# Token numbers for the first item's rows, and the combine on TensorE, in a two-layer decoder step on Trainium2

## What is computed

```python
xn = _rmsnorm(x, W['norm_ffn_g'][i])
logits = xt @ w_router                      # 1088 x 8
top_v, top_i = lax.top_k(logits, 2)
top_w = jax.nn.softmax(top_v, axis=-1)
order = jnp.argsort(top_i.reshape(-1)); tok = order // 2
xs = xt[tok]                                # rows sorted by expert
h = silu(ragged_dot(xs, wg, sizes)) * ragged_dot(xs, wu, sizes)   # 1024 -> 3584
ys = ragged_dot(h, wd, sizes) * top_w[order]
x = x + zeros.at[tok].add(ys)
g = sigmoid(_rmsnorm(x, W['norm_ple_g'][i]) @ W['ple_w_gate'][i])
x = x + g * (p[i] @ W['ple_w_proj'][i])
```

## Time and profile before

| | us |
|---|---|
| median of the runs | 5131.51 |
| the profiled execution | 5134.26 |
| its span | 5132.7 |
| PE busy in the span | 4942.7 (96%) |
| DVE busy | 3395.0 (66%) |
| ACT busy | 1597.7 (31%) |
| POOL busy | 396.3 (8%) |

### The profile page before, as it was taken

How to read it: one execution, slowest core, us unless ns; L and a number is a source line. 1 busy time by engine, 2 the same in 40 slices (tenths; PEclk the granted TensorE clock), 3 DMA queues, 4 the chain that set the end, 5 groups by cost and what they waited for, 6 DMA issues and landing times. The chain is left out here.

```text
span 5132.7 us, 86754 instructions
## 1 busy us (share of the span) xinstructions
PE 4942.7 (96%) x33110; PEld 4876.0 (95%) x33111; DVE 3395.0 (66%) x5288; ACT 1597.7 (31%) x2290; POOL 396.3 (8%) x239
## 2 busy tenths in 40 slices
PE   8999999999999999999969999999999999999968
PEld 8999999999998999999959999999999999999968
DVE  5677757444556756876557777666667777876665
ACT  2112122111113311122224444333334444443333
POOL 3110101110102021110010000000000000000020
PEclk9999999999999999999979999999999999999989
DMA  3111111111111111111035554444446555654431
GB/s 105 44 45 41 41 40 42 50 41 44 46 41 44 41 56 40 47 41 42 29 117 177 177 175 165 160 146 160 150 148 207 187 192 184 199 185 150 146 125 42
DMA packets 398841, 527.64 MB, mean 103 GB/s; under 512 B 11944, under 2 KB 353494, under 8 KB 398504
## 3 DMA queue, kind: packets, MB, share of 16 engines
q1 hardware_dynamic: 359552, 460.75, 27.3%
q0 software_dynamic: 10912, 33.94, 2.0%
q10 hardware_dynamic: 28040, 28.63, 1.7%
HBM read 494.87 MB, written 28.39 MB: 102 GB/s over the span
## 5 line engine op out<-in xcount | busy, mean ns | idle before, releaser
L1596 DVE TENSOR_TENSOR WLO<-WRAW,WHI 128x1024 fp32r<-128x1024 f32 x866 | 1071.3, 1238 | 340.8 <-ACT WHI L1192 215.9
L658 PE MATMUL PS<-XHI,WHI 128*128 128x384 f32 (+1 forms) x3648 | 1203.2, 330 | 10.6 <-DVE XLO L1843 4.5
L660 PE MATMUL PS<-XHI,WLO 128*128 128x384 f32 (+1 forms) x3648 | 1197.6, 328 | 0.0
L659 PE MATMUL PS<-XLO,WHI 128*128 128x384 f32 (+1 forms) x3648 | 1197.1, 328 | 0.0
L1192 ACT ACTIVATE WHI<-WRAW 128x1024 fp32r<-128x1024 f32 x866 | 899.1, 1051 | 892.2 <-PE PS L773 602.8
L658 PE MATMUL PS<-XSH,WHI 128*128 128x232 f32 (+6 forms) x3584 | 1058.3, 295 | 12.5 <-DVEq L2300 12.2
L659 PE MATMUL PS<-XSL,WHI 128*128 128x232 f32 (+6 forms) x3584 | 1054.7, 294 | 0.0
L660 PE MATMUL PS<-XSH,WLO 128*128 128x232 f32 (+6 forms) x3584 | 1054.6, 294 | 0.0
L658 PEld LDWEIGHTS PS<-XHI,WHI 128*128 128x128 f32 x3648 | 691.7, 190 | 13.0 <-issue 5.2
L658 PEld LDWEIGHTS PS<-XSH,WHI 128*128 128x128 f32 x3584 | 678.7, 189 | 14.4 <-DVEq L2300 13.8
L659 PEld LDWEIGHTS PS<-XLO,WHI 128*128 128x128 f32 x3648 | 691.4, 190 | 0.9
(11 more groups left out here) (361 smaller groups left out, 5956.6 us busy)
## 6 DMA issues: line engine op xcount, KB each, us to landing
WRAW<-in_moe_w_gate SPq DMA_DIRECT2D x112, 1024.0 KB, 5.0
WRAW<-in_moe_w_up SPq DMA_DIRECT2D x112, 1024.0 KB, 5.0
WRAW<-in_moe_w_down SPq DMA_DIRECT2D x112, 1024.0 KB, 5.0
WRAW<-in_w_in SPq DMA_DIRECT2D x48, 1024.0 KB, 5.2
WRAW<-in_ffn_w_gate SPq DMA_DIRECT2D x11, 1024.0 KB, 5.2
WRAW<-in_ffn_w_up SPq DMA_DIRECT2D x11, 1024.0 KB, 5.3
WRAW<-in_ffn_w_down SPq DMA_DIRECT2D x11, 1024.0 KB, 4.9
XG<-sorted_rows POOLq DMA_DIRECT2D x18, 512.0 KB, 4.6
```

Source lines behind the costliest of these rows:

```text
L658: pe.matmul(PS[:, bank, 0:n], wh, hi(k), start=(k == 0), stop=False)
L659: pe.matmul(PS[:, bank, 0:n], wh, lo(k), start=False, stop=False)
L660: ins = pe.matmul(PS[:, bank, 0:n], wl, hi(k), start=False, stop=(k == KC - 1))
L1596: v.do(dve.tensor_tensor(WLO[s][:], raw_view(conv.n // 2 % RAW, conv.n % 2, kind), WHI[s][:].bitcast(F32), ALU.subtract), conv)
```

## The change

Both stages are rewritten; items themselves stay.

- **Router weights and constants.** GpSimd loads the router weights and writes the constants when the mixers' last merged products are evicted, and VectorE folds and splits them in the output projection (d == 3). High and low halves lie side by side in RWS (16 columns), so a block's logits need two products per chunk for three; TWIN adds the two halves when logits are transposed. Logits of two blocks stand ahead of the row sums.
- **Token rows.** `rows` multiplies XHI and XLO with an identity and accumulates, so XF goes. There are nine row buffers ROWT. ScalarE evicts each tile and stores it to a new DRAM tensor token_rows (XR).
- **Token numbers.** The expert of item 0 (the first one with more than 336 tokens, or else expert 0) is found from the counts. MASK compares each token's count so far with 336 ranks; the column sums of MASK on TensorE are, per rank, the number of the token with this rank. GpSimd gathers item 0's rows from XR by these numbers, then writes the padding, then scatters.
- **List.** The nine additions become four doubling steps; 13 levels become one comparison and one reduction; the slot selector is made once instead of three times.
- **Loop for further items.** One branch on the list's count passes it by on TensorE, ScalarE and VectorE, with branch hints. Waits for the first six scatters and the padding stand ahead of the first step; the clearing of EACC goes.
- **Combine.** VectorE builds diagonal matrices DG of the weights once; TensorE multiplies both gathered rows with them and adds them to x in a main bank. Squares are summed over columns by one-column products (`sum_squares`), so `stats` goes from the gate product. The embedding of layer 1 is loaded by GpSimd at the start of the items, and transposed and split before the first gathered rows. Gather buffers go from five pairs to three.

```diff
-GATHERS = 5
+GATHERS = 3
@@ SyncE
-                if j == 1:
-                    if l == 0:
-                        sp.wait_ge(S["evicted"], Q_LAST_DOWN)
-                    else:
-                        sp.wait_ge(S["ys_out"], n_items * 48 + 48)
-                        spacer(sp)
-                    load_p(sp, l)
+                if j == 1 and l == 0:
+                    sp.wait_ge(S["evicted"], Q_LAST_DOWN)
+                    load_p(sp, [PTOK[:, i, :] for i in range(NT)], l)
@@ GpSimd
-        g.wait_ge(S["phase_clear"], 1)
+        g.wait_ge(S["evicted"], Q_MIX1)
...
+        g.wait_ge(S["rows_written"], 16 * NT)
+        g.wait_ge(S["ids_ready"], 1)
+        for c, (r0, n) in enumerate(XBLK):
+            g.indirect_dma_start(XG[0:n, c, :], None, XR[0:NTOK, :], bass.IndirectOffsetOnAxis(ap=IDS[0:n, c:c + 1], axis=0)).then_inc(S["xg_ready"], 16)
         for j, (r0, n) in enumerate(XBLK):
-            g.dma_start(XS[PAIRS + r0:PAIRS + r0 + n, :], XG[0:n, j, :]).then_inc(S["scattered"], 16)
+            g.dma_start(XS[PAIRS + r0:PAIRS + r0 + n, :], ROWT[j][0:n, :]).then_inc(S["scattered"], 16)
+        g.wait_ge(S["places_ready"], 1)
         for j in range(NT):
             n = tokens(j)
-            if j == 0:
-                g.wait_ge(S["places_ready"], 1)
-            g.wait_ge(S["rows_ready"], j + 1)
             for k in range(2):
...
-        row = g.value_load(ITEMS[0:1, L_ROW + 1:L_ROW + 2], min_val=0, max_val=PAIRS)
-        for j, (r0, n) in enumerate(XBLK):
-            g.dma_start(XG[0:n, j, :], XS[bass.ds(row + r0, n), :]).then_inc(S["xg_ready"], 16)
+        load_p(g, PTILE, 1)
@@ TensorE, router
+                pe.wait_ge(S["rw_split"], 1)
+                logits(0)
+                logits(1)
+                stats()
+                logits(2)
+                rows(0)
...
+                for j in range(NT):
+                    n = tokens(j)
+                    pe.wait_ge(S["mask_ready"], j + 1)
+                    for c in (0, 2, 1):
+                        r0, w = XBLK[c]
+                        ins = pe.matmul(PS[0:w, b, c:c + 1], MASK[0:n, j, r0:r0 + w], ONES[0:n, 0:1], start=(j == 0 and c == 0),
+                                        stop=(j == NT - 1 and c == 1))
@@ TensorE, combine
+                p_columns([t[:] for t in PTILE])
+                sums = misc_bank()
+                def sum_squares(j):
+                    n = tokens(j)
+                    for h in range(2):
+                        pe.wait_ge(S["squared"], 2 * j + h + 1)
+                        for k in range(4):
+                            ins = pe.matmul(PS[0:n, sums, j:j + 1], TC[h][:, k, 0:n], ONES[:, 0:1], start=(h == 0 and k == 0), stop=(h == 1 and k == 3))
...
-                    pe.wait_ge(S["combined"], j + 1)
+                    pe.wait_ge(S[f"gathered{j % GATHERS}"], 32 * (j // GATHERS + 1))
...
-                            ins = pe.matmul(PS[:, b, k * P:k * P + n], YG[j % GATHERS][0][0:n, c0:c0 + P], IDF[0:n, 0:n], start=False, stop=(k == 3))
+                            for e in range(2):
+                                ins = pe.matmul(PS[:, b, k * P:k * P + n], YG[j % GATHERS][e][0:n, c0:c0 + P], DG[0:n, e, j, 0:n], start=False,
+                                                stop=(k == 3 and e == 1))
+                    if j:
+                        sum_squares(j - 1)
+                sum_squares(NT - 1).then_inc(m.next(), 1)
@@ ScalarE, router
+                    act.dma_start(XR[j * P:j * P + n, :], ROWT[j][0:n, :]).then_inc(S["rows_written"], 16)
@@ VectorE, router
+                for j in range(NT):
+                    v.do(dve.tensor_scalar(MASK[:, j, :], RANKS[:], C0[:, j:j + 1], None, ALU.is_ge), masked)
@@ VectorE, combine
-                combine(0)
+                for e in range(2):
+                    v.do(dve.tensor_tensor(DG[:, e], IDF[:].unsqueeze(1).to_broadcast([P, NT, P]), TW[:, e, :].unsqueeze(2).to_broadcast([P, NT, P]), ALU.mult))
+                v.sync()
+                dve.sem_inc(S["weights_ready"], 1)
+                p_columns(PTS[1], P_SPLIT[1])
```

More of the change, by code:

```diff
@@ L292, in build @@
+    DG = at("DG", [P, 2, NT, P], F32, PH + 24576)
+    TC = [at(f"TC{i}", [P, 4, P], F32, PH + 33792 + 2048 * i) for i in range(2)]
+    assert 8192 * GATHERS <= 24576 and NT <= 9
+    assert lo + 1920 <= PH + 80000 <= END - 4 * NE
+    XR = nc.dram_tensor("token_rows", [NTOK, D], F32).ap()
     XS = nc.dram_tensor("sorted_rows", [PAIRS + CAP, D], F32).ap()
@@ L367, in spacer, with load_p @@
         eng.sem_inc(S["spacer"], 1)
-    def load_p(q, l):
+    def load_p(q, tiles, l):
         for j in range(NT):
@@ L800, in _, with p_columns @@
         for l in range(DEPTH):
+            def p_columns(tiles):
+                pe.wait_ge(S[f"p_loaded{l}"], 16 * NT)
+                for c in range(2):
+                    for t0, n in BLOCKS:
+                        b = misc_bank()
+                        for j in range(t0 // P, -(-(t0 + n) // P)):
+                            w = tokens(j)
+                            ins = pe.transpose(PS[:, b, j * P - t0:j * P - t0 + w], tiles[j][0:w, c * P:(c + 1) * P], IDF[0:w, 0:w])
+                        ins.then_inc(m.next(), 1)
             if l:
@@ L1792, in _, with p_columns @@
         tok, stage = Count(S["tok_ready"]), Count(S["stage_full"])
+        def p_columns(whole, parts):
+            for c in range(2):
+                for t0, n in BLOCKS:
+                    ps = misc_ready()
+                    v.do(dve.tensor_copy(whole[:, c, t0:t0 + n], ps[:, 0:n]), m)
+            v.sync()
+            split_branch(whole, parts)
+            dve.sem_inc(S["p_ready"], 1)
         for t_, val in ((ONES, 1.0), (EPSC, EPS)):
@@ L2353, in _ @@
                 first, second, *middle, late, last = list(groups(MOE_GROUPS))
-                with dve.Fori(0, SLOTS - NE) as it:
-                    with dve.If(it < extras):
-                        st = looped(cs, it, per)
-                        kp[0] = LOOK
-                        for k in range(KC):
-                            prepare(k)
-                        step(*first)
-                        step(*second, between=lambda u: item_out(it, u) if u < len(XBLK) else None)
-                        for s in (*middle, late, last):
-                            step(*s)
-                        leave_items(cs, st, per, extras)
+                dve.br_lt(extras, 1, on_true="dve_firsts", on_false="dve_further").branch_hint(further)
+                with nc.body("dve_further", valid_engines=[dve.engine]):
+                    with dve.Fori(0, SLOTS - NE) as it:
+                        with dve.If(it < extras):
+                            st = looped(cs, it, per)
+                            kp[0] = LOOK
+                            for k in range(KC):
+                                prepare(k)
+                            dve.wait_ge(S["rows_gone0"], 96)
+                            dve.wait_ge(S["pads_clear"], 1)
+                            step(*first)
+                            step(*second, between=lambda u: item_out(it, u) if u < len(XBLK) else None)
+                            for s in (*middle, late, last):
+                                step(*s)
+                            leave_items(cs, st, per, extras)
+                    dve.br("dve_firsts")
+                nc.switch_bb("dve_firsts")
                 for k in range(KC):
                     prepare(k)
+                dve.wait_ge(S["rows_gone0"], 96)
+                dve.wait_ge(S["pads_clear"], 1)
                 with dve.Fori(0, NE) as e:
```

411 lines of the change are left out of this document (221 added, 190 removed).

## The result

| | before | after |
|---|---|---|
| median of the runs, us | 5130.53 (12 runs) | 5144.72 (12 runs) |
| the profiled execution, us | 5134.26 | 5140.98 |
| its span, us | 5132.7 | 5139.4 |

The changed kernel is slower: the ratio of its time to that of before is 1.0027, with a 95% interval of 1.002 to 1.0035, some 14 us. That is just within the 0.3% which the prediction called about what can be told from no change, but the interval excludes a ratio of 1. I had forecast 5125.1 us and a range of 5107 to 5137. The page gives these slices for the changed kernel (busy tenths, 40 slices of 128.5 us); they hardly differ from those of before, and PE was busy for 4982.9 us where it had 4942.7.

What follows compares the result with a forecast made beforehand. TensorE bounds the kernel, at 9 tenths in nearly every slice. Router 8.6 us saved less combine 2.2 us lost gives 6.4 us saved, from the median 5131.51 to 5125.1 us; range 5107 to 5137.

Steps and rivals of the forecast that it cites:

- counts read: Router: counts at 2629.5 to 2630, where before they were read at 2642.93.
- token numbers: Router: token numbers of item 0 at 2640 to 2644, taken as 2642.
- list ready: Router: list of items ready at about 2653 against 2663.9, 11 us early.
- third convert: Router: ScalarE's third convert of weight halves starts near 2681, as before, the list's 11 us being lost to the queue.
- Logits: Router: 48 products for 72, 8 to 9.1 us for 13.65, ending near 2620.
- Row products and masks on TensorE: Router: 144 row products, 9 to 17 us, fill the waits; 27 one-column mask products cost 5.9 us.
- Weights: Router queues: weights issued at 2658.2 in mid-scatter; indirect traffic moves 0.305 MB/us against 0.087 for weights.
- The rival of sharing alike by bytes: Router queues: weights flow at 0.19 MB/us, third convert ends at 2672.7, 9.6 us more saved: 5115.5; chance 0.33.
- the rival of the clock: Combine: whole loop at 1.2 GHz costs 40 us, 5165; half the tiles give 5145; chance 0.09.
- Behind the third convert: Router: the gain is what stood between third convert and item 0's rows, 8.6 us, bounds 5 and 11.
- far jump: Router, behind the third convert: the branch past six skipped loops waits for a fetch, 3 us lost: 5128; chance 0.13.
- Combine: Combine: TensorE is the bound at 7.0 us a tile; net 2.2 us slower, bounds 4 faster and 9 slower.

Runs made afterwards that it cites:

- numbers_short: The changed kernel with the masks' products of the first tile only, so token numbers are wrong; 5133.86 us, ratio 1.0009.
- list_first: The changed kernel with places and list made on VectorE before it waits for the token numbers; 5117.16 us, ratio 0.9973.
- combine_only: The kernel before with the whole new combine and the old router; 5132.02 us, ratio 1.0003.
- list_first_squares_on_dve: The changed kernel with the list made before the numbers and the squares reduced on VectorE; 5106.72 us, ratio 0.9951.
- masks_in_bf16: list_first_squares_on_dve with masks and ones in bfloat16, one record per product of the masks; 5107.85 us, ratio 0.9958.

## Why the prediction was wrong

Step by step, from M. Times of the forecast are turned into distances from M by taking off 2609.55.

| step | forecast | after |
|---|---|---|
| row products start (logits done) | M + 10.5 | M + 10.1 |
| counts read | M + 20 | M + 28.5 |
| token numbers | M + 32.5 | M + 50.7 |
| list ready | M + 43.5 | M + 61.7 |
| weights issued | M + 48.7 | M + 65.1 |
| third convert | M + 71.5 | M + 94.5 |
| first expert product | M + 84.2 | M + 106.9 |

- **Logits.** Right.
- **Row products and masks on TensorE: the step that failed.** I gave the row products bounds of 0.06 and 0.12 us each, 9 to 17 us, wrote that they "fill the waits", and took 5.9 us for the masks' products. They took 0.11 us each in the first ones and 0.21 us in nearly all the rest, some 27 us, and the masks' products 10.3 us. The sum is 37 us where I had 15 to 23. With 3 us of transposes and counts' products between them, TensorE works without a gap for the 40 us from the logits to the numbers. It was the bound of the router, and I treated it as filler; numbers_short shows that it was on the path. This step made the numbers 18.2 us late, and of the 22.7 us by which the first expert product missed its forecast the rest is the weights: 6.6 us more from issue to convert, less 1.8 us that SyncE issued sooner behind the list (3.4 us for 5.2) and 0.3 us behind the convert. Two things lay behind this misjudged sum: the bounds left out what stands between two products that each bring their own weights, and I put the rival of the clock into the combine, where it cost little, and not into the router. The Trainium skill (TensorE: Matmul & The Clock Gate, Wait — 56ns, not 53.3ns?) has 55.6 and 106.7 ns from start to start of back-to-back products of 128 columns at the two levels; the trace has twice that, 0.11 and 0.21 us, with new weights for each product. An estimate from these two figures would make the 144 products 8 to 15 us; at the trace's 0.11 and 0.213 us they would be 16 to 31.
- **Order on TensorE.** Four blocks of row products stand ahead of the counts' products, so VectorE waited 9.30 us for sums that TensorE could have made at 2620.9, and the counts were 8 us late. In this kernel it should have cost nothing, though no run moves it: the masks were ready at 2635.1, and TensorE came to them at 2641.99.
- **Order on VectorE.** I costed the list correctly at 11 us behind the numbers (2652.36 to 2663.34), but did not ask what it had to do there. It needs the counts alone. list_first shows that this order cost 33 us up to the first expert product. This was to be read from the diff and the place of the wait.
- **Weights.** The mechanism was right and is now shown: scatter 0.311 and weights 0.074 MB/us, where I had 0.305 and 0.087 from the earlier trace rows. 29.4 us from issue to third convert, where I had 22.8. When the weights began to flow, at 2668, only some 4.3 MB of 11.7 had gone, since the queue's first 15 us (from 2653) moved 0.29 MB/us and not the 0.378 I took: I had counted on 5.8 MB left and 7.4 were. The rival of sharing alike by bytes, with its 0.19 MB/us for the weights (chance 0.33), is refuted.
- **Behind the third convert.** Right: 12.4 us to the first expert product where before had 21.1, a gain of 8.7 for 8.6. The rows of item 0 did land ahead of the third convert, by 30 us (2666.06), but at M + 64.4, where I had M + 40 to 45. No far jump shows: ScalarE's next instruction (2697.20) follows the third convert without a gap. The 2.81 us that I called a fetch in full queues stand in the earlier trace rows with the releaser "remote", and no fetch is shown there, so no run shows that rival's price.
- **Combine.** Right in sum, and partly by luck: 1.4 and 0.8 us, and 3.1 in combine_only, for 2.2. First sum 21.4 us after the last expert product (21.9 forecast). The tile was 6.3 us and not 7.0; the end at low clock (5.36 us for 32 records of squares, where 16 take 1.84 warm) and the gate product, still cold, gave part of that back. The gate product did not start warm as I wrote: the granted clock was 0.50 in its first 4 us. It came 4.5 us later after E than before, where I had 7.2, and 3.1 us came back behind it, where I had 5.0; the two errors cancel.

The router is +12 to +14 us instead of -8.6. I forecast the right mechanism in the queues from a wrong time of arrival. The range was too narrow, since it let the numbers be late by 3 us at most. Two small misreadings carry no weight: from M to the first expert product before has 92.8 us, where I wrote 92.5, and the earlier trace rows shows 2.05 us for the row sums, where I wrote 1.97.

What stays open: why M itself moves by up to 8 us between profiles of kernels whose mixing layers differ little or not at all (the changed kernel's own two profiles have 2601.66 and 2605.96), and why the clock falls with one kind of product and not with the other.

## What to carry to other kernels

When work is moved onto an engine "into its waits", add up all of it from rows of the same kind, with their weights, at both clock levels, and compare the sum with the wait; and ask of each step behind a wait whether it needs what is waited for. Where a small transfer on the path and a large one off it share the queues, their order counts more than their times: the same weights were converted 16 us sooner, counted from M, when they were issued 4 us ahead of the gathers (list_first_squares_on_dve) than when they went out 0.8 us behind them (masks_in_bf16), and making the large one's trigger earlier can lose as much as it wins. Measure from a landmark close to the change when profiles scatter by more than the effect.

## What the runs showed of the hardware

- The granted clock fell to 1.2 GHz in the midst of work without a gap, some 14.6 us after M in the changed kernel, with products of 128 columns in the reduced format fp32r that each load their own weights. From 2616 to 2652 it averaged 0.50 to 0.56 in all eight profiles of kernels with them, and it was 1.00 with fp32 products in their place. I had taken a falling clock for a matter of waits.
- An fp32 product of 128 columns (two records) takes 0.223 us at 2.4 GHz, and an fp32r product 0.11 at 2.4 and 0.213 at 1.2.
- One-column fp32 products cost 0.107 us a record at 2.4 GHz (16 records in 1.70 us, from the start at 4971.67 to that of the next product) and 0.19 at 1.2 (10.26 us for 54). With 128 columns a record takes 0.11, so the number of columns hardly counts here; the change adds 27 of these products to the router and 72 to the combine. The same 27 products in bfloat16 took 0.05 us each at 1.2 GHz (1.37 us).
